# A hybrid pooling and mLSTM layer on one core: the value projection with tokens stationary and weight columns moving

## The reference, cut to what matters

```python
h = modulate(layer_norm(x), sh1, sc1)
proj = h @ p['w_in']
xp = proj[..., :o1]                                  # 512 columns: pooling mixer
q = proj[..., o1:o1 + MLSTM_W]
k = proj[..., o1 + MLSTM_W:o1 + 2 * MLSTM_W]
v = proj[..., o1 + 2 * MLSTM_W:o1 + 3 * MLSTM_W]     # 512 columns
o = proj[..., o1 + 3 * MLSTM_W:o1 + 4 * MLSTM_W]
...
pool_out = pool_mixer(xp.reshape(B, rows, cols, POOL_W), p['w_pool'], p['pool_scale'])
ml_out, st_new = mlstm_mixer(q, k, v, o, gates, ...)
...
num = a_inter * (q @ C) + s @ v                      # per chunk of tokens, in the scan
```

## Time and profile before

| | us |
|---|---|
| median of 3 runs | 1322.42 (1319.21, 1322.42, 1322.7) |
| the profiled execution, its own time | 1322.36 |
| its span in the profile | 1320.6 |
| PE busy | 1257.7 (95%) |
| DVE busy | 1051.0 (80%) |
| POOL busy | 666.7 (50%) |
| ACT busy | 591.8 (45%) |

### The profile page before, as it was taken

One profiled execution on the slowest core, in us unless ns is written; L12 is line 12 of the kernel. 1 busy time (PEld: TensorE's weight loads), 2 busy tenths in 40 slices (PEclk: granted clock), 3 DMA queues, 4 the chain that ended last, 5 costly groups with the idle time before them and its releaser, 6 DMA issues.

```text
span 1320.6 us, 21789 instructions
## 1 busy us (share of the span) xinstructions
PE 1257.7 (95%) x7739; PEld 1163.4 (88%) x7739; DVE 1051.0 (80%) x1520; ACT 591.8 (45%) x1023; POOL 666.7 (50%) x503
## 2 busy tenths in 40 slices
PE   5899999999998899989999999999999999999996
PEld 3689999999987778888999999999999988888885
DVE  8565799894577689879887878787885779879898
ACT  6443223455445724555444444444444455345430
POOL 1000999743333011319887888797877874200011
PEclk9899999999999999999999999999999999999998
DMA  9522332483325532212354445444443579946892
GB/s 341 164 83 78 101 87 80 120 231 82 104 80 192 189 101 104 74 44 90 106 194 139 157 143 179 153 142 158 168 156 130 190 247 353 360 137 186 288 327 108
DMA packets 164851, 210.28 MB, mean 159 GB/s; under 512 B 10567, under 2 KB 102819, under 8 KB 164515
## 3 DMA queue, kind: packets, MB, share of 16 engines
q1 hardware_dynamic: 164286, 204.47, 47.4%
q0 software_dynamic: 288, 4.72, 0.9%
q10 hardware_dynamic: 197, 0.06, 0.0%
HBM read 161.49 MB, written 47.72 MB: 158 GB/s over the span
## 4 chain that ended last, share of the span: by engine, by line
PE 50%; POOL 2%; DVE 1%; issue 1%; ACT 0%; POOLq 0%
PE ps L1591 11%; PE ps L1589 11%; PE ps L1590 11%; PE ps L1622 6%; PE ps L1623 6%; PE ps L1624 6%; POOL tlo L2227 0%; POOL ulo L2227 0%; POOL xlo L2227 0%; POOL dwlo L2227 0%; POOL xwlo L2227 0%; PE ps L1152 0%; POOL wsum L2428 0%; DVE z L3233 0%; DVE z L3232 0%
## 5 line engine op out<-in xcount | busy, mean ns | idle before, releaser
L3047 DVE SCALAR_TENSOR_TENSOR ps<-gs,taps,ps 128x945 f32<-128x945 f32 (+2 forms) x176 | 215.7, 1226 | 10.0 <-ACT ps L2005 4.6
L2370 POOL TENSOR_TENSOR rstd<-mv,neghalf 128x1 f32<-128x1 f32 x27 | 25.1, 930 | 258.1 <-DVE mv L3224 156.9
L1241 PE MATMUL ps<-h1hi,whi 128*128 128x384 f32 x432 | 152.6, 353 | 2.8 <-DVE wlo L2567 2.8
L1241 PE MATMUL ps<-h1hi,wlo 128*128 128x384 f32 x432 | 145.5, 337 | 0.0
L1241 PE MATMUL ps<-h1lo,whi 128*128 128x384 f32 x432 | 145.2, 336 | 0.0
L1622 PE MATMUL ps<-dwhi,uhi 128*128 128x512 f32 x290 | 113.1, 390 | 1.3 <-POOL dwlo L2227 1.3
L1624 PE MATMUL ps<-dwhi,ulo 128*128 128x512 f32 x290 | 112.8, 389 | 0.0
L1623 PE MATMUL ps<-dwlo,uhi 128*128 128x512 f32 x290 | 112.8, 389 | 0.0
L1589 PE MATMUL ps<-thi,xhi 128*128 128x288 f32 x320 | 94.3, 295 | 2.0 <-issue 1.1
L2227 POOL TENSOR_TENSOR wlo<-raw,whi 128x512 fp32r<-128x512 f32 x44 | 62.0, 1411 | 66.2 <-ACT whi L1694 30.3
L1591 PE MATMUL ps<-thi,wlo 128*128 128x288 f32 x320 | 94.4, 295 | 0.0
(11 more groups left out here) (434 smaller groups left out, 4019.1 us busy)
## 6 DMA issues: line engine op xcount, KB each, us to landing
raw<-in_w_up SPq DMA_DIRECT2D x78, 256.0 KB, 4.6
u_rows<-val SPq DMA_DIRECT2D x22, 576.0 KB, 2.9
adaw<-in_w_ada SPq DMA_DIRECT2D x24, 512.0 KB, 4.1
st<-in_w_down SPq DMA_DIRECT2D x22, 512.0 KB, 4.2
t_rows<-st SPq DMA_DIRECT2D x11, 1024.0 KB, 4.6
raw<-in_w_in SPq DMA_DIRECT2D x40, 256.0 KB, 4.5
w_raw<-in_w_down SPq DMA_DIRECT2D x33, 256.0 KB, 5.3
v_raw<-u_rows SPq DMA_DIRECT2D x33, 256.0 KB, 5.0
```

What stands on the lines that cost most here:

```text
L1241: last = mm(ps[:, bank, 0:GN], a[:, n % 2, k * P:(k + 1) * P], b[:, kk, grp(g)], start=(kk == 0 and a is whi and b is h1hi), stop=(kk == K ...
L2370: tt(rstd[:, j % 4, :], mv[:, j % 4, 1:2], neghalf[:, 0, :], ALU.pow).then_inc(rstd_ready, 1)
L3047: step(stt(a3[:, ro, co], g3[:, ri, ci], taps[:, tap:tap + 1], a3[:, ro, co], ALU.mult, ALU.add), 2 + m)
```

## The change

The eight value units become eight blocks of 128 features by all 512 value columns, each one contiguous row of 2 KB in memory (`V_FIRST` = 8, `V_LAST` = 16). `v_tile(t)` takes 128 tokens stationary and 512 weight columns moving, over 8 blocks of features and 3 products, into one bank: 24 matmuls, and 9 such tiles. The result has the tokens on the partitions, and ACT copies it straight into `v1`, 9 copies of 128x512. The 36 transposes, their 12 copies and the four tile copies of the values are gone. `v_tile(0)` to `v_tile(7)` stand in the place of units 8 to 15, and `v_tile(8)` behind the last.

Since every token tile reads all eight blocks, all eight must be split before `v_tile(0)` ends and stay until `v_tile(8)`. Six of the pairs lie in space that is free at that time (`vw`), two in `whi` and `wlo`. `LO_TURN` sets the order of the splits on ACT and DVE, and the loads move up on SP. In turn lo(16) and lo(17) come at unit 15, and unit 16 waits until the last value tile has been copied out (`v_ready` at `NT`).

```diff
+V_FIRST, V_LAST = 2 * H, 4 * H
+LO_TURN = {4: (6,), 5: (7,), 6: (8, 9, 10), 7: (11, 12, 13), 8: (14, 15)}
-for _n in range(12):
-    JOBS[10 + _n] = ("v", _n // 3, _n % 3)
...
+        vw = [(place(f"vwhi{k}", [P, UC], at, F32R), place(f"vwlo{k}", [P, UC], at + 4 * UC, F32R))
+              for k, at in enumerate([qk_at + 8 * UC * k for k in range(4)] + [work_at + 1024 + 8 * UC * k for k in range(2)])]
+        def vsplit(k):
+
+            return vw[k] if k < 6 else (whi[:, k % 2, :], wlo[:, k % 2, :])
...
             def load_proj(n):
                 wait_raw_free(sp, n)
+                if V_FIRST <= n < V_LAST:
+                    k = n - V_FIRST
+                    sp.dma_start(raw[:, n % RAWN, :], w_in[0, k * P:(k + 1) * P, 3 * H * P:4 * H * P]).then_inc(raw_in[n % RAWN], 16)
+                    return
...
-                if n + RAWN < U_OUT:
-                    load_proj(n + RAWN)
+                for unit in {4: (8,), 5: (9, 10), 6: (11, 12), 7: (13, 14, 15)}.get(n, () if 8 <= n < 12 else (n + RAWN,)):
+                    if unit < U_OUT:
+                        load_proj(unit)
...
+            def v_tile(t, between=None):
+
+                order = list(range(KT)) if t < NT - 1 else [6, 7] + list(range(6))
+                if t == 0:
+                    pe.wait_ge(tile_out, tile_count(2))
+                elif t == NG:
+                    pe.wait_ge(tile_out, tile_count(3))
+                elif t >= 2 * NG:
+                    pe.wait_ge(v_ready, t - 2 * NG + 1)
+                for m, k in enumerate(order):
+                    if t == 0:
+                        wait_lo(pe, V_FIRST + k)
+                    w_hi, w_lo = [x[:, :] for x in vsplit(k)]
+                    for a, w in ((h1hi, w_hi), (h1hi, w_lo), (h1lo, w_hi)):
+                        last = mm(ps[:, t % (2 * NG), :], a[:, k, chunk(t)], w,
+                                  start=(m == 0 and a is h1hi and w is w_hi), stop=(m == KT - 1 and a is h1lo))
+                    if t == NT - 1:
+                        last.then_inc(pe_unit, 1)
+                    if between is not None and m in (2, 5):
+                        between(m // 3)
+                if t < NT - 1:
+                    last.then_inc(pe_v, 1)
...
+                if V_FIRST <= n < V_LAST:
+                    v_tile(n - V_FIRST, lambda g: jobs_after(n, g))
+                    jobs_after(n, NG - 1)
+                    if n == V_LAST - 1:
+                        v_tile(NT - 1)
+                    continue
                 wait_lo(pe, n)
                 if n % 2 == 0:
-                    pe.wait_ge(tile_out, tile - 1)
+                    if n == V_LAST:
+                        pe.wait_ge(v_ready, NT)
+                    else:
+                        pe.wait_ge(tile_out, tile_count(tile - 2))
...
+            def v_hi(n):
+
+                raw_wait(act, n)
+                act.wait_ge(pe_unit, 4 if n < V_LAST - 2 else n - 7)
+                fn(vsplit(n - V_FIRST)[0][:, :], raw[:, n % RAWN, :], ACT.Copy).then_inc(whi_ready, 1)
...
+                fn(v1[:, t, :, 0:P], ps[:, t % (2 * NG), :].rearrange("p (h n) -> p h n", h=H), ACT.Copy).then_inc(v_ready, 1)
...
-                hi(n + 2)
-                if n % 2:
+                if n < V_FIRST - 2:
+                    hi(n + 2)
+                elif n < V_FIRST:
+                    for unit in LO_TURN[n] + ((14,) if n == 7 else ()):
+                        v_hi(unit)
+                elif n == V_LAST - 1:
+                    v_evac(NT - 2)
+                    hi_after_v(V_LAST)
+                    hi_after_v(V_LAST + 1)
+                    v_evac(NT - 1)
+                elif n >= V_LAST:
+                    hi(n + 2)
...
+                if n == V_FIRST - 1:
+                    v_hi(V_LAST - 1)
...
-                if n + 2 < U_LO:
-                    lo(n + 2)
+                for unit in LO_TURN.get(n, () if n < V_LAST else (n + 2,)):
+                    if unit < U_LO:
+                        lo(unit)
...
+                if n == V_LAST - 1:
+                    lo(V_LAST)
+                    lo(V_LAST + 1)
```

More of the change, by code:

```diff
@@ L337, in pair_of, with tile_count @@
             return x.rearrange("p (a n) -> p a n", a=2)
+        vw = [(place(f"vwhi{k}", [P, UC], at, F32R), place(f"vwlo{k}", [P, UC], at + 4 * UC, F32R))
+              for k, at in enumerate([qk_at + 8 * UC * k for k in range(4)] + [work_at + 1024 + 8 * UC * k for k in range(2)])]
+        assert 16 * UC * 2 <= 4 * H * T and 1024 + 16 * UC <= 8 * T
+        def vsplit(k):
+            return vw[k] if k < 6 else (whi[:, k % 2, :], wlo[:, k % 2, :])
+        def tile_count(tile):
+            return tile + 1 if tile < H else tile + 1 - H
         def xslot(n):
@@ L1265, in gate_job @@
                     mm(ps[:, 7, 3 * P:4 * P], bc(gcol[:, 4:5], [P, P]), ident[:, :], start=True, stop=True).then_inc(pe_tok, 1)
[L1267 to L1277, removed]
+            def v_tile(t, between=None):
[19 more added lines that the diff above has]
+                    last.then_inc(pe_v, 1)
             def pool_job(j):
                 g, part = divmod(j, 3)
-                pe.wait_ge(v_ready, 13)
+                pe.wait_ge(tok_ready, 1)
                 pe.wait_ge(wpl_in, 16)
@@ L1298, in _ @@
                         last.then_inc(pe_unit, 1)
[L1299 to L1303, removed]
-                        gate_job(GATE_JOBS[n, g])
+                    jobs_after(n, g)
                     if g == 0 and POOL_FIRST <= n < POOL_LAST:
                         pool_job(2 * (n - POOL_FIRST))
-                if n in JOBS:
-                    misc_job(JOBS[n])
                 if POOL_FIRST <= n < POOL_LAST:
@@ L1803, in _ @@
                     fn(Wr[:, :], Wr[:, :], ACT.Ln, bias=1.0).then_inc(ln_ready, 1)
-                hi(n + 2)
-                if n % 2:
+                if n < V_FIRST - 2:
[10 more added lines that the diff above has]
+                    hi(n + 2)
+                if n % 2 and not V_FIRST <= n < V_LAST:
                     tile = n // 2
@@ L1809, in _ @@
                         dst = qk[:, H + tile, :]
-                    elif tile < 2 * H:
-                        dst = qk[:, tile - H, :]
                     else:
@@ L2694, in gate_chain5 @@
                 dve.wait_ge(pe_ada, N_ADA1)
-                v.memset(v1[:, :, :, P:P + 1], 1.0).then_inc(v_ready, 1)
+                v.memset(v1[:, :, :, P:P + 1], 1.0).then_inc(v_ones, 1)
             def conv(j):
                 tile = 2 * H + j
-                dve.wait_ge(tile_out, tile + 1)
-                if j < H:
-                    dve.wait_ge(pe_v, 3 * (j + 1))
-                else:
+                dve.wait_ge(tile_out, tile_count(tile))
+                if j >= H:
                     dve.wait_ge(pe_pool, 3 * (j - H + 1))
```

46 lines of the change are left out of this document (27 added, 19 removed).

## The result

The changed kernel took 1327.12 us (median of 9 runs, 1324.72 to 1331.55), the kernel before 1321.54 us (9 runs, 1318.17 to 1325.12) on the same chip. The ratio is 1.0041, 95% interval [1.0026, 1.0056], which is 5.4 us slower, where 1.1 us faster was forecast. The prediction was wrong; the time lies 1.1 us above its range.

A forecast was written before the change was run, and what follows sets the result against it. TensorE hardly stops; from unit 18 DVE's queue also limits. Of 5.2 us removed from TensorE, 1.6 go into new waits, 2.1 are hidden, 0.4 wait for DVE: 1322.4 - 1.1 = 1321.3 us, range 1317.5 to 1326.0.

The forecast's parts named there:

- Matmuls: Value stretch on TensorE: 216 matmuls of 512 columns, 0.227 us apart, take 49.0 against 49.9 us; other end +0.7.
- The wait for lo(15): In `v_tile(0)`, TensorE waits 0.7 us for block 15's low part, from nothing to 1.8 us.
- The copy of `v_tile(8)`: Ahead of unit 16, TensorE waits 0.9 us, fully exposed, for ACT to copy the last value tile.
- TensorE's own sum: By TensorE's work and new waits alone, unit 16 starts at 174.5, against 176.0 before.
- Transposes: TensorE loses 4.3 us of transposes; 2.2 in units 10 to 15 count, those of units 16 to 20 are hidden.
- Ada units ahead of lo(16): DVE's 18 operations of ada units 16 to 24 take 28.5 us, so unit 16 starts at 174.9, 1.1 us earlier.
- the run of ada operations gets longer: Rival, DVE ahead of lo(16): from 29.6 us the change loses; over 4 us needs mean above 2.1 us; chance 0.08.
- The coupling: DVE's queue from unit 16's end sets unit 21's start: lo(18), lo(21) and unit 21 move by the same 1.1 us.

The follow-up runs named there:

- with the gap filled: Changed kernel with 20 unread matmuls ahead of unit 16's wait and 12 ahead of unit 21's: ratio 1.0060 against the kernel before.
- without the chain: GpSimd's pooling arithmetic left out: changed kernel 0.9952, kernel before 0.9976; changed kernel with four added TensorE gaps 1.0144, with these filled by unread matmuls 1.0090.
- reordering alone: Changed kernel, lo(16), lo(17) ahead of ada 23 and ada 25, 26 ahead of lo(18), lo(19): 1.0001; also first three convolutions behind later low parts: 0.9978.
- the low parts first: Changed kernel with DVE forming lo(16) and lo(17) ahead of ada unit 23: ratio 1.0028 against the kernel before.

## Why the prediction was wrong, point by point

- *Matmuls.* Taken 0.227 us apart; nine tiles started 5.53 us apart are 0.230. Cost 0.8 us above the forecast, inside its bounds. The argument for the lower of the two distances, the same 0.013 us over the column time, didn't hold: here it is 0.017.
- *The wait for lo(15)*, put at 0.7 us, didn't show: TensorE has no wait of note in the first value tile. GpSimd began at 127.53, with the offset of 0.78 some 1.8 us ahead of the forecast 128.5.
- *The copy of `v_tile(8)`*, put at 0.9 us: 0.78 where lo(16) was early. Right. TensorE's own sum, 174.5 for unit 16, is right too: with lo(16) early and the offset taken off it started at 174.8. That is luck in part: the matmuls cost 0.8 us more and the wait for lo(15) 0.7 less.
- *Transposes.* That those of units 16 to 20 are hidden was right for the changed kernel: unit 21 waited 2.76 instead of 1.52 us, and unit 20 another 0.57 us for lo(20). The forecast was 3 to 4 us; the slow clock of unit 16 used up TensorE's slack too.
- *Ada units ahead of lo(16)*: this is the step that failed. The prediction gave DVE "the 18 operations of ada units 16 to 24, which took 24.6 + 3.0 + 0.9 = 28.5 us". They took 32.0 us: 26.2 instead of 24.6 for the 14 plain ones, 2.3 instead of 0.9 and 3.5 instead of 3.0 for the first ones of the blocks. `ada2_cols` had ended at 144.9 with the offset off (145.0 forecast), so the whole miss is in the run behind it: with the offset off, unit 16 started at 178.1, where 174.9 was forecast. I carried durations from the earlier trace rows to another alignment with GpSimd's chain, though the four operations that start a block had shown how much that matters. The rival "the run of ada operations gets longer" was the right one, given 0.08; its threshold of 29.6 us was passed. But its price was too low as well: 32.0 - 29.6 is a loss of 2.4 us, and for one over 4 us it wanted a mean of 2.1 us for a plain operation, which was 1.91. The other 3 us of the loss lie behind unit 16's start.
- *"DVE then idles until unit 16 ends, so lo(18), lo(21) and unit 21 move by the same 1.1 us."* The coupling held: from the start of lo(18) to the end of lo(21) DVE took 27.76 us (190.26 to 218.02), against 27.58 before. What it was fed with was wrong, and this is the larger part. Unit 16 began 2.1 us later than before, and its length, which the prediction took as fixed, grew by 2.4 us at the slow clock; lo(18) started 4.4 us later, lo(21) ended 4.5 us later. The account of DVE says the same from its side. From its restart at 145.80 to the end of lo(21) at 218.02 it had 63.3 us of work and 9.0 of idle time; before, from 147.57 to 212.70, 62.4 and 2.8, with three low parts more. It restarts 2.5 us earlier (offset off), and loses 6.2 to idle time and 0.9 to longer work: 4.6 us later at lo(21).
- *The granted clock* was in no term. Behind the wait of 4.1 us unit 16 ran 10.4 instead of 8.0 us. What it adds to the measured 5.4 us isn't settled by the sum: with the gap filled and the clock kept the kernel got no faster, since lo(20) then waited for TensorE's unit 18 and lo(21) ended 0.4 us earlier only; without the chain the same clock cost 1.5 to 2 us for each gap. At unit 21, where TensorE is full from then on, the 1.5 us (20.40 us against 3 x 6.24 = 18.7 and a short job for the three units) I read as lost in full; less the wait of 0.36 us at unit 23 and the transpose that are gone, they make up the +0.8 (this is read from the rows; no run took this gap away by itself).

Shown by the runs is that DVE's order beside the chain, not TensorE's work, makes the loss: reordering alone takes back 5.3 us (1.0041 - 1.0001), then 8.3 (1.0041 - 0.9978). The Trainium skill (SBUF — State Buffer, "Who interferes with whom") calls the port pair that DVE and GpSimd share an exclusive lock, and has a DVE instruction with two SBUF inputs contend with a GpSimd instruction that reads SBUF. The runs agree as far as they go: conv(0) took 3.13 us with no chain, and 7.31, 9.01, 10.03 and 12.16 us at four alignments with it (the changed kernel, the kernel before, and two of the orders).

## What to carry to other kernels

Durations of VectorE operations beside a busy GpSimd held here only for the alignment in which they were measured (28.5 against 32.0 us for the same 18); where a run of such operations is put in front of something that the bound engine waits for, price it by the range of its single operations, and put what is waited for first. When work goes from the bound engine, ask whether the next engine has idle time in its queue behind a dependence: there the saving is lost. Moving the awaited work forward and filling that idle time gave back 5.3 us here, where the change itself is worth 3.4 us. And price a new wait of TensorE by the clock behind it too: one of 4 us cost 1.5 to 2 us beyond its length, while those of 1.2 to 1.6 us cost their length alone.

## What the hardware showed

- Twelve waits of TensorE between 2.76 and 6.59 us stand in the stretches compared here. Behind eleven of them the next 5 us or so had a granted clock of 0.50 to 0.67 (0.66 after 2.76, 0.59 after 5.63, 0.67 after 6.59 us). Behind one of 3.22 us it was 1.00, from 211.12 to 216.10, and so it was behind another of 3.22 us much later, at 472.65 in the kernel with the gaps filled. Two waits of 2.81 and 2.82 us near 585 in other traces had 0.66 behind them. So the length of a wait alone didn't decide it. Behind waits of 1.20, 1.28, 1.52 and 1.63 us the clock was 1.00.
- Both kernels differ from execution to execution ahead of the change: the granted clock of the first 120 us was 0.96 in the profile of the kernel before and 0.93 in that of it without the chain, and the value stretch began between 121.1 and 124.5 us.
- Single DVE operations beside the chain changed their time several fold with the alignment, but the queue from lo(18) to lo(21) kept its sum in three traces: 27.39 us busy before, 27.59 in the changed kernel, 27.56 with the gaps filled. With the same queue begun 5.6 us earlier in the stretch (the low parts first) it was 29.54.
